# DeltaNet's block inverse: five of its levels on diagonal blocks of 64 rows, with the work around them rearranged

## The reference

```
# per head and chunk of c rows; k, q have unit norm; gc = cumsum(g); gamma = exp(gc_t - gc_s) for s <= t
low  = where(s < t, (k * beta) @ k.T * gamma, 0)
u, w = solve(I + low, [v * beta, k * beta * exp(gc)])       # unit lower triangular
attn = where(s <= t, q @ k.T * gamma, 0)                    # q scaled by dk ** -0.5
v_new = u - w @ S
o     = (q * exp(gc)) @ S + attn @ v_new
S     = S * exp(gc_last) + (k * exp(gc_last - gc)).T @ v_new
```

## Time and profile before

| | us |
|---|---|
| three timed runs | 1852.32, 1856.49, 1857.23 (median 1856.49) |
| the profiled execution | 1843.68 |
| its span | 1842.0 |
| PE busy in the span | 1751.6 (95%) |
| PEld, DVE, ACT, POOL busy | 1627.3, 1013.5, 721.5, 402.5 |
| largest group: products of line 674 | 1162.5 |
| DeltaNet, one prompt chunk | 50.15 to 50.49 |

### The profile page before, as it was taken

One profiled execution on the slowest core, in us unless ns is written; L12 is line 12 of the kernel. 1 busy time (PEld: TensorE's weight loads), 2 busy tenths in 40 slices (PEclk: granted clock), 3 DMA queues, 4 the chain that ended last, 5 costly groups with the idle time before them and its releaser, 6 DMA issues. The chain is left out here.

```text
span 1842.0 us, 36269 instructions
## 1 busy us (share of the span) xinstructions
PE 1751.6 (95%) x13404; PEld 1627.3 (88%) x13404; DVE 1013.5 (55%) x1848; ACT 721.5 (39%) x1239; POOL 402.5 (22%) x580
## 2 busy tenths in 40 slices
PE   8999899999799999999999999799899999999997
PEld 6999788888498999999998998555598999999997
DVE  4763455552537776777225433576537667668224
ACT  4342333331436433436224311556446333336222
POOL 1553344353000222221000000343400222221000
PEclk9999999998899999999999999999999999999999
DMA  4222111100521222222222224889721222222222
GB/s 175 80 80 80 71 35 35 34 20 1 194 81 58 80 83 88 80 91 98 91 91 69 80 69 171 282 306 312 254 91 58 80 80 80 82 89 73 96 91 87
DMA packets 78367, 188.61 MB, mean 102 GB/s; under 512 B 9442, under 2 KB 25186, under 8 KB 77906
## 3 DMA queue, kind: packets, MB, share of 16 engines
q1 hardware_dynamic: 71618, 168.47, 27.0%
q0 software_dynamic: 6672, 19.10, 3.1%
HBM read 176.00 MB, written 11.55 MB: 102 GB/s over the span
## 5 line engine op out<-in xcount | busy, mean ns | idle before, releaser
L674 PE MATMUL PB<-parts,wparts 128*128 128x288 f32 x8664 | 1162.5, 296 | 20.6 <-DVE wparts L643 9.2
L674 PEld LDWEIGHTS PB<-parts,wparts 128*128 128x128 f32 x8664 | 1157.1, 190 | 24.6 <-DVE wparts L643 19.3
L633 ACT ACTIVATE wparts<-ring 128x1024 fp32r<-128x1024 f32 x198 | 209.8, 1060 | 675.8 <-PE PB L674 675.1
L643 DVE TENSOR_TENSOR wparts<-ring,wparts 128x1024 fp32r<-128x1024 f32 x174 | 213.0, 1225 | 272.4 <-ACT wparts L633 262.9
L1033 POOL COPY cnew<-arena 128x2 f32 (+1 forms) x106 | 115.0, 1085 | 337.8 <-DVE arena L958 335.0
L970 DVE SCALAR_TENSOR_TENSOR arena<-arena,ffw 128x512 f32<-128x512 f32 x176 | 133.7, 760 | 19.3 <-DVE arena L971 12.8
L684 PE MATMUL PB<-parts,wparts 128*128 128x288 f32 x648 | 104.8, 310 | 3.9 <-DVE parts L513 3.3
L955 DVE TENSOR_TENSOR arena<-PB,stats 128x288 f32<-128x288 f32 x88 | 40.3, 458 | 121.6 <-PE PB L674 115.0
L684 PEld LDWEIGHTS PB<-parts,wparts 128*128 128x128 f32 x648 | 91.0, 188 | 12.8 <-DVE parts L513 7.3
L1009 DVE SCALAR_TENSOR_TENSOR arena<-arena,dnw 128x512 f32<-128x512 f32 x54 | 58.0, 1075 | 32.8 <-ACT arena L908 27.6
L932 ACT ACTIVATE arena<-arena,ffw 128x512 f32<-128x512 f32 x88 | 63.8, 725 | 27.5 <-issue 15.5
(11 more groups left out here) (299 smaller groups left out, 2090.4 us busy)
## 6 DMA issues: line engine op xcount, KB each, us to landing
ring<-in_w SPq DMA_DIRECT2D x198, 512.0 KB, 3.2
arena<-in_kpages SPq DMA_DIRECT2D x64, 256.0 KB, 6.1
arena<-in_vpages SPq DMA_DIRECT2D x64, 256.0 KB, 5.0
arena<-in_kpages POOLq DMA_DIRECT2D x64, 128.0 KB, 2.7
arena<-in_vpages POOLq DMA_DIRECT2D x64, 128.0 KB, 5.6
membuf<-in_w SPq DMA_DIRECT2D x8, 512.0 KB, 6.1
arena<-in_state_dn SPq DMA_DIRECT2D x6, 512.0 KB, 5.0
o_dns_s<-arena SPq DMA_DIRECT2D x6, 512.0 KB, 3.9
```

What stands on the lines that cost most here:

```text
L633: nc.scalar.activation(wparts[:, 0, k, :], ring[:, k, :], ACT.Copy).then_inc(hi_ready, 1)
L643: nc.vector.tensor_tensor(wparts[:, 1, k, :], ring[:, k, :], wparts[:, 0, k, :].bitcast(F32), ALU.subtract).then_inc(lo_ready, 1)
L674: last = nc.tensor.matmul(dst(b), wparts[:, part, k, block * P:(block + 1) * P], x[:, row_, b * HALF:(b + 1) * HALF], start=start and part ...
```

## The change

- *Levels 1 to 5* work on the two diagonal blocks of 64 rows alone. Below level 6 everything outside them is zero. A head's two blocks are stored side by side in partitions 0 to 63 and 64 to 127, 64 columns wide (`LTb`, `M1b`, `BTb`, `TXb`), and `blocks()` issues for each head two 64x64 products on opposite corners of the array, into the two partition halves of one PSUM bank. `x` and `xt` of a group share a bank, and one DVE operation of 384 columns subtracts both.
- *Start of the inverse.* `lc` multiplies only the diagonal blocks by beta, in two operations on 64 partitions. `tt0` is then three DVE operations on 192 columns: times a mask that holds -1 inside blocks of two, plus the identity, and a transposition of 32x32 blocks on DVE. The transposition on TensorE and ACT's copy are gone. The whole of `LT` (`lb`), which level 6 needs, follows behind level 1.
- *Widening.* Behind level 5, `full` spreads `TXb` back to 128 columns (`em` into `Tm`, `et` into `TT`), group by group; level 6 is as before.
- *Queries.* `qn` moves from DVE to POOL; its scale goes into ACT's logarithm, which is split in two.
- *Values.* `vt` stands behind level 5 on TensorE, into banks 6 and 7, and `vb` behind the widening on DVE. `kd`, `wk` move to levels 2 and 3.
- *POOL's masks* are 192 columns for a group at level 1 and 384 for both groups at levels 2 to 5, in two buffers by turns.
- *The loop* over chunks is written out, with constants in place of registers.
- *The sample chunk* does the same with one block of 64 rows and without level 6: `vt` behind level 1, `et` at the end.

```
+        BTb = TT.rearrange("p h n -> p (h n)").rearrange("p (l h n) -> p l h n", l=2, h=DN_H)
+        TXb = [M1.rearrange("p h n -> p (h n)")[:, 384 * g:384 * g + 384].rearrange("p (x h n) -> p x h n", x=2, h=3)
+               for g in range(2)]
...
-            pe = "gb0 gb1 ss0 ss1 bb0 bb1 kk0 kq0 kk1 kt0 kt1 kq1 vt0 t00 vt1 t01 "
+            pe = "gb0 gb1 ss0 ss1 bb0 bb1 kk0 kk1 kt0 kt1 kq0 kq1 "
...
+            def blocks(out, left, right):
                 for h in range(3):
+                    for i in range(T // 64):
+                        b = slice(64 * i, 64 * i + 64)
+                        last = nc.tensor.matmul(out[b, h, :], left[b, h, :], right[b, h, :], start=True, stop=True)
+                return last
...
+                if l <= 5:
+                    for g in G:
+                        wait("pool", f"bt1_{g}" if l == 1 else f"bt{l}")
+                        wait("dve", f"tt0{g}" if l == 1 else f"x{l - 1}_{g}")
+                        blocks(bank_b(2 * g, T), BTb[0:T, (l - 1) % 2, 3 * g:3 * g + 3, :], TXb[g][0:T, 0, :, :]).then_inc(...)
+                    for g in G:
+                        wait("act", f"m{l}_{g}")
...
+                        if l < levels - 1:
+                            blocks(bank_b(2 * g + 1, T), TXb[g][0:T, 1, :, :], M1b[g][0:T, 0, :, :])
+                        blocks(bank_b(2 * g + 1, T, 1), M1b[g][0:T, 0, :, :], TXb[g][0:T, 1, :, :]).then_inc(...)
+                    if l == (1 if sample else 5):
+                        vt(0)
+                        vt(1)
+                    continue
...
-                nc.scalar.activation(f, PB[:, 2 * g:2 * g + 2, ...], ACT.Ln, bias=epsc)
+                nc.scalar.activation(f[:, 0, :, :], bank(2 * g, P, T), ACT.Ln, bias=qepsc, scale=float(P))
+                nc.scalar.activation(f[:, 1, :, :], bank(2 * g + 1, P, T), ACT.Ln, bias=epsc)
...
+            def lc(g):
+                for i in range(T // 64):
+                    b = slice(64 * i, 64 * i + 64)
+                    last = nc.vector.tensor_tensor(LTb[b, 3 * g:3 * g + 3, :], heads(LT, g, T, T)[b, :, b],
+                                                   bank(4 + g, T, T)[b, :, b], ALU.mult)
...
+                nc.vector.tensor_tensor(tx[:, 1, :, :], heads_b(LTb, g, T), small_m[0:T, 0, :]..., ALU.mult)
+                nc.vector.tensor_tensor(tx[:, 1, :, :], tx[:, 1, :, :], small_m[0:T, 6, :]..., ALU.add)
+                nc.vector.transpose(tx[:, 0, :, :]..., tx[:, 1, :, :]...)
...
+            def full(name, dst, x, g):
+                wait("dve", f"x{5 if not sample else levels - 1}_{g}")
+                nc.vector.tensor_tensor(heads(dst, g, T, T)..., TXb[g][0:T, x, :, :]..., block2[0:T, 0:T]..., ALU.mult)
...
-            for step, g in ((kn_, 0), (qn_, 0), (kn_, 1), (lt, 0), (lb, 0), (qn_, 1), (lt, 1), (lb, 1), (tt0, 0), (tt0, 1),
-                            (vb_, 0), (at, 0), (vb_, 1), (at, 1)):
+            for step, g in ((kn_, 0), (kn_, 1), (lt, 0), (lc, 0), (tt0, 0), (lt, 1), (lc, 1), (tt0, 1), (at, 0), (at, 1)):
...
+                        nc.vector.tensor_tensor(tx, tx, PB[0:T, 2 * g + 1, 192 * x0:384]..., ALU.subtract)
+                        if l == 5:
+                            full("em", Tm, 0, g)
+                            full("et", TT, 1, g)
...
+            pool.wait_ge(bs["dve"].sem, bs["dve"].at("oz1", bt))
+            for g in G:
+                wait("act", f"r{g}")
+                nc.gpsimd.tensor_tensor(heads(qn, g, P, T), qcols(0, g), heads(rq, g, P, T), ALU.mult)
...
-            with eng.Fori(0, NCH // 2) as i:
+            for i in range(NCH // 2):
```

More of the change, by code:

```diff
@@ L1213, in kt @@
                 last.then_inc(S_, mark(f"kt{g}"))
+            vt_bank = 4 if sample else 6
             def vt(g):
                 wait("pool", "vst")
-                wait("dve", f"lb{g}")
+                wait("dve", f"lc{g}" if sample else f"wk{g}")
                 for h in range(3):
-                    last = nc.tensor.transpose(bank(4 + g, T, P)[:, h, :], vst[:, 3 * g + h, 0:T], ident)
+                    last = nc.tensor.transpose(bank(vt_bank + g, T, P)[:, h, :], vst[:, 3 * g + h, 0:T], ident)
@@ L1240, in dn_pe @@
                     for h in range(3 * g, 3 * g + 3):
[L1241 removed]
+                        last = nc.tensor.matmul(bank(2 * g, T, T)[:, h - 3 * g, :], BT[0:T, h, 0:T], Tm[0:T, h, 0:T],
                                                 start=True, stop=True)
@@ L1245, in dn_pe @@
                     wait("act", f"m{l}_{g}")
-                    wait("dve", f"at{g}" if l == 1 else f"xt{l - 1}_{g}")
+                    wait("dve", f"et{g}")
                     if l < levels - 1:
                         for h in range(3 * g, 3 * g + 3):
-                            last = nc.tensor.matmul(bank(2 + g, T, T)[:, h - 3 * g, :], TT[0:T, h, 0:T], M1[0:T, h, 0:T],
+                            last = nc.tensor.matmul(bank(2 * g + 1, T, T)[:, h - 3 * g, :], TT[0:T, h, 0:T], M1[0:T, h, 0:T],
                                                     start=True, stop=True)
@@ L1256, in dn_pe @@
             for g in G:
-                wait("dve", f"xt{levels - 1}_{g}")
+                wait("dve", f"et{g}" if sample else f"xt{levels - 1}_{g}")
                 wait("dve", f"wk{g}")
@@ L1362, in dn_act @@
                     wait("pe", f"m{l}_{g}")
-                    nc.scalar.activation(heads(M1, g, T, T), bank(g, T, T), ACT.Copy).then_inc(S_, mark(f"m{l}_{g}"))
+                    if l == 6:
+                        wait("dve", f"et{g}")
+                    if l <= 5:
+                        dst, src = M1b[g][0:T, 0, :, :], bank_b(2 * g, T)
+                    else:
+                        dst, src = heads(M1, g, T, T), bank(2 * g, T, T)
+                    nc.scalar.activation(dst, src, ACT.Copy).then_inc(S_, mark(f"m{l}_{g}"))
             if not sample:
@@ L1431, in vb_ @@
             def vb_(g):
                 wait("pe", f"vt{g}")
-                nc.vector.tensor_tensor(heads(vb, g, T, P), bank(4 + g, T, P), bc(0, g), ALU.mult).then_inc(S_, mark(f"vb{g}"))
+                nc.vector.tensor_tensor(heads(vb, g, T, P), bank((4 if sample else 6) + g, T, P), bc(0, g), ALU.mult).then_inc(S_, mark(f"vb{g}"))
             def at(g):
@@ L1506, in dn_dve, with dn_pool @@
                         step(g)
-        def dn_pool(pool, s, c, before, levels, T, sample, vcols):
+        def dn_pool(pool, s, c, before, levels, T, sample, vcols, qcols):
             ct, c = c, 0 if sample else c
```

175 lines of the change are left out of this document (110 added, 65 removed).

## The result

The changed kernel is faster, by less than half of what was forecast: 1846.81 us (six runs, 1844.69 to 1849.31) beside 1857.16 for the kernel before, ratio 0.9945 [0.9932, 0.9957]. A second series (ten runs, 1849.33 beside 1855.35) gave 0.9966 [0.9950, 0.9982]. That is 10 and 6 us for a forecast of 24; the time lies inside the range given, well away from its likeliest value.

A forecast was written before the change was run, and what follows sets the result against it. TensorE's stream was taken to bound levels 2 to 6, a four-engine chain paced by VectorE and GpSimd the front. Chunks 28.4, sample -2.4 and clock -2 gave 24 us: 1856.49 to 1832 us, range 1812 to 1852.

The forecast's parts named there:

- The levels: Levels of the inverse in prompt chunks: opposite corners run at once, so a level takes 2.63 us for 4.27.
- The front and the tail: Prompt chunk before level 3: 3.2 us gained; from level 6 to the product with the keys: 0.4 us lost.
- Widening puts four VectorE operations (0.46 apart): Between levels 5 and 6 of a prompt chunk: level 6's first product waits for one operation, +0.65 us.
- six dependent operations of 0.35 to 0.45: Sample chunk on VectorE, behind the beta product: six operations for two, part of a 2.4 us loss there.
- the 41 to 46: Length of a prompt chunk in us: any chunk outside this would show the forecast wrong; 43 us expected.
- One such dip in every second chunk: Half-clock stretches of 3.4 us after the new front's hole, at most 1.7 us each: 2 us lost with overlap.
- 28.4 - 2.4 - 2 = 24: Whole kernel, us: four prompt chunks gain 28.4, sample chunk loses 2.4, clock loses 2; 24 faster.
- Corners in turns: Rival 1, levels: the corners take turns, a level takes 4.36 us against 4.27; 1.6 us slower, 1858; chance 0.10.
- a falling clock that eats everything: Rival 2: half-clock stretches at every hole fill the levels; 13.6 us slower, 1870; chance 0.07.
- more than half a dozen: Sign of rival 2: that many stretches at 0.50 clock between 207 and 380 us.
- No collisions: Rival 3: GpSimd never holds VectorE up and the clock stays; 32 us faster, 1824; chance 0.20.
- nothing, or 1 us either way: Writing out the loop: removes register work before waits, adds two chunk bodies of code; no effect, or 1 us.

The follow-up runs named there:

- the version with both waits: Changed kernel with GpSimd's memory-weight units after chunk 4's second widening, and its later sample work after the second group's start of the inverse: 1837.16 us, ratio 0.9902.
- the profile with the old sample chunk: Changed kernel with GpSimd's units behind chunk 4's widening and the sample chunk in the earlier kernel's form: 1827.24 us, ratio 0.9842.
- the unrolled kernel: Kernel before with only the loop over chunks written out with constants: 1858.09 us, ratio 1.0007.
- a filled hole: Version with both waits plus three unread products on TensorE between the groups' first level 1 products in each prompt chunk: 1836.73 us, ratio 0.9884.

## Why the forecast was wrong

*The levels: right.* The rule weighed against it (the Trainium skill, TensorEngine Tiling (Array Packing), section Restrictions and Gotchas: row tiles cannot share a bank at one time) does not hold for opposite corners: both halves of a product go to one bank, and 72 records, whose loads would take 4.2 us in a row, run within a level of 2.70 us (4.27 in the earlier trace rows, 2.63 forecast):

```profile
228.19 2.46 PEld L1256 LDWEIGHTS PB<-arena 64*64 64x64 f32 x72 [0.24 <-issue]
...
229.52 1.25 DVE L1521 TENSOR_TENSOR arena<-arena,PB 128x384 f32<-128x384 f32 x2 [0.52 <-PE PB L1256]
...
230.89 2.46 PEld L1256 LDWEIGHTS PB<-arena 64*64 64x64 f32 x72 [0.24 <-issue]
```

*The front and the tail: right.* Level 1's first products start 10.1 and 13.0 us into the chunk (10.3 and 13.4 forecast), and the block transpose takes 0.38 us (0.36). Level 3's first product, the first group's, starts at 227.49, 17.9 us into the chunk (17.9): 3.2 us gained for 3.2. Level 3 to level 6 takes 8.7 us (8.5), level 6 to the keys 3.7 (3.7). Together 6.9 us in the first chunk for 7.1.

```profile
227.49 0.46 PEld L1256 LDWEIGHTS PB<-arena 64*64 64x64 f32 x12
...
236.19 0.74 PEld L1282 LDWEIGHTS PB<-arena 128*128 128x128 f32 x6
...
239.91 1.59 PEld L1301 LDWEIGHTS PB<-arena 128*128 128x128 f32 x12
```

*The failed step* is "Widening puts four VectorE operations (0.46 apart)", taken as the same in all four chunks, and "six dependent operations of 0.35 to 0.45" in the sample. I had seen in the earlier trace rows that GpSimd holds such an operation (1.33 us for 0.55), and let it count once for each of three operations in the front, where the measured start was even a little earlier. I did not ask which GpSimd work stands beside the other new operations of this kind. Four units at the end of chunk 4 (1.9 us each alone, 2.2 for two that a widening preceded), and a mask, the decayed queries and another unit in the sample, did: 5.6 and 4.5 us by taking them away, of which 4.3 and 3.75 are the stretched operations. So chunk 4 lasted 50.2 us, outside the 41 to 46 that the prediction had set as its limits. The Trainium skill, SBUF — State Buffer, section "SBUF: two separate sides", has the rule that I left out: a VectorE operation with two SBUF inputs and a GpSimd operation that reads SBUF exclude each other for a whole instruction. Chunk 4 agrees, one unit for each of the three held widenings. The sample shows more: three queued GpSimd instructions passed the waiting operation (400.71 to 404.49).

*The clock* was mis-sized too. "One such dip in every second chunk" became one in each of chunks 2 to 4 (1.2 us each), and the sample chunk, where I counted none, ran at half clock. Of its 10.4 us, 3.5 are the added steps (2.4 forecast), 4.5 the hold and the other 2.4 the clock; by the version with both waits (18.9 us) the hold is 3.8 and the clock 3.1. What TensorE did before it fell, in chunk 2: a stretch with 1.1 us busy of 3.4, and then

```profile
262.50:265.90 3.40, 1.09 (x20) 0.86 (x18) 3.12 (x8) 0.33 (x1) 1.55 (x2) 1.00 0.00 0
265.90:269.30 3.40, 3.40 (x64) 3.40 (x66) 1.45 (x3) 0.33 (x1) 1.28 (x2) 0.50 0.02 5
```

The sum by measured terms, first profile against first profile: chunks 7.0 + 5.7 + 5.8 + 0.3 = 18.8, sample -10.4, behind it -2.8: 5.6 us, the stage's 5.4 but for rounding, for 28.4 - 2.4 - 2 = 24. The term behind the sample was not in the forecast; half clock goes on there for 7.9 us (415.0 to 422.9), but what the term comes from is not shown. The intervals of the two timed series are 8 to 13 and 3 to 9 us; the stage's 5.4 lies in the second alone, and what the first has beyond it stays open.

*The rivals.* Corners in turns are out, and so is a falling clock that eats everything: four half-clock stretches stand between 207 and 380 us, where "more than half a dozen" were its sign. No collisions (32 us) was wrong in the other direction: collisions were the case. With the holds and the sample's reorganisation taken out, the change is worth 26 to 30 us (1829.37 for 1855.35, 1827.24 for 1856.83). That is near the 28.4 us that the chunks alone were forecast to give, in part by luck: in the profiles of these two versions the chunks give 26.1 and 24.4 us, and some 4 us come from behind the sample chunk's product with the keys.

## What to carry to other kernels

Before an operation is given two SBUF operands on VectorE, look up what GpSimd runs beside it in *every* place where it will stand, the last pass and the remainder case too: a stretched operation looks busy, not idle. A form that pays on full tiles need not pay on the remainder; keep the old form there if its chain is shorter. Where executions differ by 10 us for other reasons, compare stages, and take a second profile of the kernel before.

## What was not expected of the hardware

The large projections have two cadences. Records of 288 columns follow each other every 133.3 ns (28.80 us for 216) throughout the second profile of before, and every 130.0 ns (28.08 us) from 611 to 836 us in the first. In these traces the cadence changes at half-clock stretches, where another stage lies between, and at waits of TensorE of 2 to 3 us at full clock (near 831, 845 and 1685 us in the profile with the old sample chunk); what chooses it stays open. Line 674 is busy 6.8 us longer in one of those two profiles than in the other.

Half clock at the same place of a chunk, some 13 us into it, came in three of four chunks of the changed kernel's first profile, in all of the unrolled kernel's and in none of the looped one's, with nearly the same work in front. So the dips that the new form shows may come in part from writing out the loop, which the prediction put at nothing, or 1 us either way; why stays open. That a filled hole removed them in chunks 2 to 4 is shown by one profile and seen again in the two others with it.
